# Decay products placed behind the factors' bank, and masks and high parts reordered, in two recurrent layers

## The chip, the cores and the metric

The kernel runs on one core of a Trainium2 chip. The metric is the device time of one execution in microseconds (us), lower is better. Five engines work side by side, each in its own program order, and meet only at semaphores: PE (TensorE, matrix products into eight PSUM banks), ACT (ScalarE), DVE (VectorE), POOL (GpSimd) and SP, which issues the weight transfers.

## The reference

A sequence of 256 tokens of width 1024 goes through four layers (a recurrent mixer, stick-breaking attention, sparse attention, a recurrent mixer again), each with a gated feed-forward block, and then through two hybrid attention layers. All is in float32. The change lies in the recurrent mixer, which runs twice, in layer 0 (n = 0) and layer 3 (n = 1):

```python
def rwkv7_time_mix(h, v_first, mix, w_rkv, ..., v_res):
    shifted = jnp.pad(h, ((0, 0), (1, 0), (0, 0)))[:, :-1]
    xm = h[:, :, None, :] + (shifted - h)[:, :, None, :] * mix
    rkv = jnp.einsum('bsjd,jde->bsje', xm[:, :, :3], w_rkv)
    r, k, v = rkv[:, :, 0], rkv[:, :, 1], rkv[:, :, 2]
    ...
    if v_res is not None:
        v0, v1, v2 = v_res
        v = v + (v_first - v) * jax.nn.sigmoid(v0 + (xv @ v1) @ v2)
    ...
    def step(state, inp):
        r_t, w_t, k_t, v_t, kk_t, a_t = inp
        sa = jnp.einsum('bhvk,bhk->bhv', state, kk_t)
        state = (state * w_t[:, :, None, :]
                 - sa[..., None] * (kk_t * a_t)[:, :, None, :]
                 + v_t[..., None] * k_t[:, :, None, :])
        return state, jnp.einsum('bhvk,bhk->bhv', state, r_t)
```

## The kernel before

The recurrence is computed in four chunks of 64 tokens. For each chunk and head the kernel builds a 64 x 64 lower triangular matrix from products of decayed keys and inverts it by doubling: blocks of 2, 4, 8, 16 and 32 (LEVELS). Around this work stand the three big products with `w_rkv`, in the order keys (m = 1), queries (m = 0), values (m = 2). Every weight block of 256 columns is used as a high and a low part: ACT rounds the high part (`hi`, line 444), DVE subtracts for the low part (`lo`, line 454), PE multiplies with both (lines 384 to 386). The inputs of these products are split the same way. For the values' input DVE mixes tokens into the slots of buffer 12 (`prepare(2, ...)`, line 2355), ACT rounds them (`rounded(2, ...)`, line 1589: the high parts) and DVE subtracts (line 2241).

The order on each engine is written out by hand, and each engine works strictly in it. Around the change it is as follows.

- PE: third queries' block `full(0, 1, 2)`; the gate's and the values' factors "gv" (lines 772 and 773), which ACT reads out with a sigmoid (line 1687) and, in layer 3, a copy (line 1689); the decay products "pb" (line 790, one pair of banks for each j of 0 and 1); the first half of the fourth queries' block; the decay products "bp" (line 790 again, operands exchanged); the second half of that block; then for each level first products "xs" (line 814) and transposes "turn" (line 823), half a block of the values, second products "low" (line 814), the other half. The first products need "bp" as ACT has copied it (line 1701) and the triangle as DVE has masked it (line 2469).
- DVE: the decayed keys (lines 2395 and 2396), which "pb" multiplies; two low parts; the values' mixed input; the four masked copies of "pb" into the triangle (line 2469); low parts.
- ACT: two high parts of weights; the third queries' block out of its bank (line 1597); the sigmoid; the four high parts of the values' input; the four copies of "bp"; high parts; the fourth queries' block; then the copies of "xs" (line 1710) and of "turn" (line 1701), the latter into buffer 12.

PSUM banks go round a ring. `bank(e, key, *free)` takes the next and makes PE wait for what frees its last content. From "pb" to the end of the inversion the ring has banks 1 to 7 (`cur["first"] = 1`), and bank 0 is kept for the blocks of queries and values. `cur["bank"]` is set to the bank after which the ring goes on. Behind the inversion it goes over all eight again, from the bank after the last one used.

The lines that set the place of "pb" and that take a bank:

```python
            i = cur["first"] + cur["bank"] % (8 - cur["first"])
            cur["bank"] += 1
            for ev in bank_free.get(i, ()):
                e.wait_ge(*at(*ev))
...
            cur["first"], cur["bank"] = 1, bank_of["full", n, 0, 2]
            for j in range(2):
                gram("pb", j, Pm, Bt_)
```

Of the kernel before, what the change touches and what calls it, by code (L numbers as in the profile page):

```python
# [88 lines left out]
class Book:  # L89
# [8 lines left out]
    def up(self, name, *keys):  # L98
        self.n[name] += 1
        for k in keys:  # L100
            self.value[name, k] = self.n[name]
        return self.sems[name], 1
# [7 lines left out]
    def at(self, name, key):  # L110
        return self.sems[name], 1 if self.rehearsal else self.value[name, key]
# [9 lines left out]
def build(nc, A, out_ap, OFF, NCONST):  # L121
    ctx = ExitStack()
    with ctx:
# [13 lines left out]
        BUF = {}  # L137
# [3 lines left out]
        HH, HL, XH, XL, XHe, XLe = (t[:, i, :] for t in (H_, X_, E_) for i in range(2))  # L141
# [16 lines left out]
        up, at, mark = book.up, book.at, book.mark  # L158
# [6 lines left out]
        def C(name, a=0, b=None):  # L165
            o, n = OFF[name]
            return CT[:, o + a:o + (n if b is None else b)]
# [4 lines left out]
        def FM(i):  # L172
            return BUF[i][:, :].rearrange("p (k t) -> p k t", k=KD)

        def TM(i):
            return BUF[i][:, :].rearrange("p (j c) -> p j c", j=2)
# [4 lines left out]
        def low8(m):  # L181
            return C(f"low{m}").bitcast(I32).unsqueeze(1).to_broadcast([P, 8, HD])

        def q8(ap):
            return ap.rearrange("p (q t) -> p q t", q=8)
# [18 lines left out]
        def pair(t, g):  # L204
            return FR(t)[:, 2 * g:2 * g + 2, :]
# [102 lines left out]
        cur, bank_of, bank_free = {}, {}, {}  # L308

        def PS(*key):  # L310
            return PSB[bank_of[key]]
# [126 lines left out]
        def hi(e, count=2):  # L438
            for u in range(cur["hi"], min(cur["hi"] + count, len(units))):
                j, k0, kn = units[u]  # L440
                e.wait_ge(s_raw[j % RAW], landed[j])
                if u >= UNITS:
                    e.wait_ge(book.sems["unit"], u - UNITS + 1)
                e.activation(wh[:, u % UNITS, 0:kn * 256], raw[:, j % RAW, k0 * 256:(k0 + kn) * 256], ACT.Copy).then_inc(*up("hi"))  # L444
                cur["hi"] = u + 1

        def lo(e, count=2):
            for u in range(cur["lo"], min(cur["lo"] + count, len(units))):
                j, k0, kn = units[u]
                e.wait_ge(book.sems["hi"], u + 1)  # L450
                e.wait_ge(s_raw[j % RAW], landed[j])
                if u >= UNITS:
                    e.wait_ge(book.sems["unit"], u - UNITS + 1)
                e.tensor_tensor(wl[:, u % UNITS, 0:kn * 256], raw[:, j % RAW, k0 * 256:(k0 + kn) * 256],  # L454
                                wh[:, u % UNITS, 0:kn * 256].bitcast(F32), ALU.subtract).then_inc(*up("lo"))
                cur["lo"] = u + 1
# [33 lines left out]
        def col(name, k, a=0):  # L490
            c = COL[name] + a * KD + k
            return cols[:, c:c + 1]
# [57 lines left out]
        def mix_slot(g):  # L550
            return FM(12)[:, 2 * (g % 2):2 * (g % 2) + 2, :]
# [165 lines left out]
        def pe_rwkv(e, layer, n):  # L717
# [9 lines left out]
            def block_halves(m, p, g):  # L727
                key, free = ("full", n, m, g), ("dve", ("vmix", n, g)) if n and m == 2 else ("act", ("full", n, m, g))
                ready = [[("dve", ("xml", n, m, k // 2))] for k in range(KD)] if g == 0 else None
                o = kept_bank(e, 0, key, free)  # L730
                for k0, kn, u in next_units(KD):
                    fm_unit(e, key, o, KD, k0, kn, u, parts_of(*((HH, HL), (XH, XL))[p]), ready)
                    yield
# [72 lines left out]
            groups = [(j, par) for j in range(2) for par in range(2)]  # L806
# [46 lines left out]
                    i.then_inc(*up("mm", ("v2", n, g)))  # L853

            last_read = block_halves(0, 1, 3)
            cur["first"], cur["bank"] = 1, bank_of["full", n, 0, 2]
            for j in range(2):
                gram("pb", j, Pm, Bt_)
            next(last_read)
# [719 lines left out]
        def act_rwkv(e, layer, n):  # L1579
# [5 lines left out]
            def rounded(m, hi_, g, *free):  # L1585
                for ev in free:
                    e.wait_ge(*at(*ev))
                e.wait_ge(*at("dve", ("xm", n, m, g)))
                e.activation(pair(hi_, g), mix_slot(g), ACT.Copy).then_inc(*up("act", ("xmh", n, m, g)))
# [97 lines left out]
            e.activation(sg[0:32, 1, :], PS("gv", n)[0:32, 0:S], ACT.Sigmoid).then_inc(*up("act", ("gv", n)))  # L1687
            if n:
                e.activation(lor[32:64, :], PS("gv", n)[32:64, 0:S], ACT.Copy).then_inc(*up("act", ("gv", n)))
            for g in range(4):  # L1690
                rounded(2, HH, g, ("unit", ("full", n, 1, 3)))
            term, V = FM(4), TM(2)
            Y, pTM, bTM, kTM = FM(6), TM(3), TM(1), TM(8)
            Lk, Un, Tt, At = (BUF[b][:, :].rearrange("p (j r x) -> p j r x", j=2, r=2) for b in (14, 0, 12, 1))
# [2 lines left out]
            groups = [(j, par) for j in range(2) for par in range(2)]  # L1697

            def copy_out(key, dst, scale=1.0):
                e.wait_ge(*at("mm", key))  # L1700
                e.activation(dst, PS(*key)[:, :], ACT.Copy, scale=scale).then_inc(*up("act", key))
# [5 lines left out]
            def quarters_out(key, m, j, dst, scale=1.0):  # L1707
                for a in range(2):
                    e.wait_ge(*at("mm", (key, n, m, j, 1)))
                    e.activation(dst[:, j, :, a, :], q8(PS(key, n, m, j, a)[:, :]), ACT.Copy, scale=scale).then_inc(*up("act", (key, n, m, j, a)))  # L1710

            def turned(m):
                for j in range(2):
                    for r in range(2):
                        copy_out(("turn", n, m, j, r), Tt[:, j, r, :])

            for j, par in groups:
                copy_out(("bp", n, j, par), At[:, j, par, :])
            hi(e, 1)
            for g in range(4):  # L1720
                hi(e, 1)
                if g == 0:
                    evac(0, 3, R_)
                elif n == 0:
                    evac(2, g - 1, v_)
                for j in range(2):
                    quarters_out("xs", LEVELS[g], j, X1)
                turned(LEVELS[g] // 2)
                if g == 2:
                    e.wait_ge(*at("mm", ("gv", n)))  # L1730
                    e.wait_ge(*at("dve", ("PB", n, 1)))
                    e.activation(BUF[0][:, :].rearrange("p (q t) -> p q t", t=HD), C("eye").unsqueeze(1).to_broadcast([P, 32, HD]),
                                 ACT.Copy).then_inc(*up("act", ("eye", n)))
                hi(e, 1)
                if n and g == 0:
                    for q in range(4):
                        sigmoids("v2", q, "rw_v0", vmix, 0)
# [585 lines left out]
        def dve_rwkv(e, layer, n):  # L2323
# [17 lines left out]
            def prepare(m, hl, *free):  # L2341

                def rest(g):
                    dve_lo_part(e, mix_slot(g), (pair(hl[0], g), pair(hl[1], g)), ("act", ("xmh", n, m, g)), ("xml", n, m, g))

                for ev in free:
                    e.wait_ge(*at(*ev))
                for g in range(4):
                    e.wait_ge(*at("dve", ("step", n, g)))
                    e.wait_ge(*at("act", ("d0", n, g)))  # L2350
                    if g >= 2:
                        e.wait_ge(*at("dve", ("xml", n, m, g - 2)))
                    for u in range(2):
                        k = 2 * g + u
                        i = e.scalar_tensor_tensor(out=mix_slot(g)[:, u, :], in0=d[:, k, :], scalar=col("rw_mix", k, n * 6 + m), in1=h[:, k, :],
                                                   op0=ALU.mult, op1=ALU.add)
                    i.then_inc(*up("dve", ("xm", n, m, g)))
                    if g:
                        rest(g - 1)
                rest(3)  # L2360
# [92 lines left out]
            erase_and_write(0)  # L2453
            erase_and_write(1)
            lo(e)
            prepare(2, (HH, HL), ("unit", ("full", n, 1, 3)), ("dve", ("k2", n, 3)))
            BR, KR, Lk, Un = (BUF[b][:, :].rearrange("p (j r x) -> p j r x", j=2, r=2) for b in (9, 11, 14, 0))
            T, Xw = GQ(6), GQ(0)
# [2 lines left out]
            def masked(kind, j, par, dst, name):  # L2461
                e.wait_ge(*at("mm", (kind, n, j, par)))
                e.tensor_tensor(q8(dst[:, j, par, :]), q8(PS(kind, n, j, par)[:, :]), bc8(name), ALU.mult).then_inc(*up("dve", (kind, n, j, par)))

            groups = [(j, par) for j in range(2) for par in range(2)]
            for j, par in groups:
                e.wait_ge(*at("act", ("minus eye", n, j)))
                e.wait_ge(*at("mm", ("pb", n, j, par)))
                e.copy_predicated(q8(BUF[6][:, (2 * j + par) * 512:(2 * j + par) * 512 + 512]), low8(1),
                                  q8(PS("pb", n, j, par)[:, :])).then_inc(*up("dve", ("pb", n, j, par), ("low", n, 1, j, par)))  # L2470

            def level(key, m, dst):
                for j in range(2):
# [698 lines left out]
```

## Time and profile before

| | |
|---|---|
| median of 3 runs | 1830.6 us (1829.88 to 1832.39) |
| the profiled execution | 1837.71 us |
| its span, first to last instruction | 1835.9 us |
| mean granted PE clock | 0.984 |
| busy: PE, DVE, ACT, POOL | 1762.6, 1288.7, 1034.0, 69.2 us |

The span is 1.8 us short of that execution's own time, and the execution is 0.4% above the median of the runs. A timeline lists instructions in order of time, equal ones merged into one row with a count: start, length from the first's start to the last's end, engine, line, operation, output and inputs, and in brackets the idle time of the engine before it with what ended it. The ends of PE's instructions are modelled, and successive ones overlap.

### The profile page before, as it was taken

To read this page: it belongs to the slowest core of one execution; us is meant where nothing else is said; L and a number is where in the kernel's file an instruction comes from. 1 tells how busy PE (TensorE), PEld (TensorE's weight loads), DVE (VectorE), ACT (ScalarE), POOL (GpSimd) and SP (SyncE) were. 2 spreads that over 40 slices of the span, in tenths; PEclk is the share of its full clock that TensorE was granted. 3 is DMA by queue.
4 is the path that set the end of the run, shared out by engine and by line. 5 is a ranking of instruction groups with operands and counts; after the bars stand their busy time and mean duration, and the time that the engine had idled before them with its cause. 6 is when DMAs were issued, how large, how long until landed. Compare 5 with 4: busy or idle time off the path is not lost.

```text
span 1835.9 us, 40364 instructions
## 1 busy us (share of the span) xinstructions
PE 1762.6 (96%) x17129; PEld 1594.8 (87%) x17129; DVE 1288.7 (70%) x1897; ACT 1034.0 (56%) x1608; POOL 69.2 (4%) x54
## 2 busy tenths in 40 slices
PE   7899899999999999999999999899999999998997
PEld 6798798889989888987888889798798888997997
DVE  7853468965457995598788757663579956875874
ACT  6856365554556555456655548754555544564564
POOL 0001000000000000214000000001000000000000
PEclk9999999999999999999999999999999999998998
DMA  7320157755436875542495653210368655453541
GB/s 222 119 86 4 52 183 253 251 190 181 138 115 229 275 234 179 161 141 79 143 267 188 200 173 115 85 49 4 103 226 278 225 182 167 138 161 103 159 144 64
DMA packets 276298, 287.60 MB, mean 157 GB/s; under 512 B 15304, under 2 KB 261944, under 8 KB 276120
## 3 DMA queue, kind: packets, MB, share of 16 engines
q1 hardware_dynamic: 272824, 283.92, 47.8%
q8 instruction: 136, 2.23, 0.5%
q10 hardware_dynamic: 3296, 1.11, 0.3%
q14 instruction: 42, 0.34, 0.1%
HBM read 283.96 MB, written 1.05 MB: 155 GB/s over the span
## 4 chain that ended last, share of the span: by engine, by line
PE 89%; DVE 5%; ACT 3%; issue 2%; DMA 0%; SPq 0%; DVEq 0%; ACTq 0%
PE ps L407 24%; PE ps L408 13%; PE ps L384 10%; PE ps L385 9%; PE ps L386 9%; PE ps L814 2%; PE ps L422 2%; PE ps L423 2%; PE ps L424 2%; PE ps L790 1%; PE ps L799 1%; DVE wl L454 1%; PE ps L983 1%; PE ps L714 1%; PE ps L634 1%
## 5 line engine op out<-in xcount | busy, mean ns | idle before, releaser
L454 DVE TENSOR_TENSOR wl<-raw,wh 128x1024 fp32r<-128x1024 f32 x484 | 582.3, 1227 | 243.7 <-ACT wh L444 240.9
L444 ACT ACTIVATE wh<-raw 128x1024 fp32r<-128x1024 f32 x484 | 497.4, 1041 | 376.6 <-PE ps L408 189.8
L407 PE MATMUL ps<-HH,wh 128*128 128x512 f32 x1408 | 490.8, 391 | 0.8 <-DVE HH L2870 0.8
L408 PE MATMUL ps<-HH,wl 128*128 128x256 f32 x1408 | 397.0, 282 | 0.0
L407 PEld LDWEIGHTS ps<-HH,wh 128*128 128x128 f32 x1408 | 264.3, 188 | 56.4 <-DVE HH L2870 1.1
L384 PE MATMUL ps<-HH,wh 128*128 128x256 f32 x928 | 269.3, 290 | 6.9 <-DVE HH L2672 6.4
L408 PEld LDWEIGHTS ps<-HH,wl 128*128 128x128 f32 x1408 | 266.1, 189 | 0.1
L386 PE MATMUL ps<-HH,wl 128*128 128x256 f32 x928 | 261.4, 282 | 0.8 <-issue 0.8
L385 PE MATMUL ps<-HH,wh 128*128 128x256 f32 x928 | 261.6, 282 | 0.0
L384 PEld LDWEIGHTS ps<-HH,wh 128*128 128x128 f32 x928 | 177.0, 191 | 15.8 <-DVE HH L2672 4.9
L385 PEld LDWEIGHTS ps<-HH,wh 128*128 128x128 f32 x928 | 177.1, 191 | 1.3 <-issue 1.2
L386 PEld LDWEIGHTS ps<-HH,wl 128*128 128x128 f32 x928 | 177.0, 191 | 1.0 <-issue 1.0
L384 PE MATMUL ps<-XH,wh 128*128 128x256 f32 x512 | 146.9, 287 | 10.5 <-DVE XH L2241 6.9
L385 PE MATMUL ps<-XH,wh 128*128 128x256 f32 x512 | 144.6, 282 | 0.0
L386 PE MATMUL ps<-XH,wl 128*128 128x256 f32 x512 | 144.3, 282 | 0.0
L407 PE MATMUL ps<-XE,wh 128*128 128x512 f32 x336 | 117.0, 390 | 0.0
L384 PEld LDWEIGHTS ps<-XH,wh 128*128 128x128 f32 x512 | 97.8, 191 | 14.1 <-DVE XH L2241 6.5
L385 PEld LDWEIGHTS ps<-XH,wh 128*128 128x128 f32 x512 | 97.9, 191 | 0.0
L386 PEld LDWEIGHTS ps<-XH,wl 128*128 128x128 f32 x512 | 97.9, 191 | 0.0
L408 PE MATMUL ps<-XE,wl 128*128 128x256 f32 x336 | 94.8, 282 | 0.0
L422 PE MATMUL ps<-wh,HH 128*128 128x256 f32 x256 | 74.9, 293 | 0.0
L3052 POOL TENSOR_TENSOR B<-B 128x512 f32<-128x512 f32 x20 | 26.0, 1301 | 1294.4 <-ACT B L1499 1294.3
(337 smaller groups left out, 3090.4 us busy)
## 6 DMA issues: line engine op xcount, KB each, us to landing
raw<-in_ffn_w_gu_dram SPq DMA_DIRECT2D x88, 1024.0 KB, 5.3
raw<-in_ffn_w_down_dram SPq DMA_DIRECT2D x32, 1024.0 KB, 5.2
raw<-in_w_in_dram SPq DMA_DIRECT2D x32, 1024.0 KB, 5.5
raw<-in_rw_w_rkv_dram SPq DMA_DIRECT2D x24, 1024.0 KB, 5.2
B<-in_w_ada_dram SPq DMA_DIRECT2D x24, 1024.0 KB, 7.5
raw<-in_ds_w_in_dram SPq DMA_DIRECT2D x14, 1024.0 KB, 5.2
raw<-in_ffn_w_down_dram SPq DMA_DIRECT2D x16, 768.0 KB, 4.4
raw<-in_sb_w_qkv_dram SPq DMA_DIRECT2D x12, 1024.0 KB, 5.2
```

The costliest lines, as they stand in the source:

```text
L384: e.matmul(om, h_[:, k, c], xh_, start=m == 0 and k0 + k == 0, stop=False, skip_group_check=True)
L385: e.matmul(om, h_[:, k, c], xl_, start=False, stop=False, skip_group_check=True)
L386: i = e.matmul(om, l_[:, k, c], xh_, start=False, stop=k0 + k == kt - 1, skip_group_check=True)
L407: e.matmul(o[:, m, :], h_[:, k, c], x_, start=k0 + k == 0, stop=False, skip_group_check=True)
L408: i = e.matmul(o[:, m, 0:S], l_[:, k, c], x_[:, 0, :], start=False, stop=k0 + k == kt - 1, skip_group_check=True)
L422: e.matmul(oj, xh_[:, c], h_[:, k, :], start=j == 0 and k0 + k == 0, stop=False, skip_group_check=True)
L423: e.matmul(oj, xl_[:, c], h_[:, k, :], start=False, stop=False, skip_group_check=True)
L424: i = e.matmul(oj, xh_[:, c], l_[:, k, :], start=False, stop=k0 + k == KD - 1, skip_group_check=True)
L444: e.activation(wh[:, u % UNITS, 0:kn * 256], raw[:, j % RAW, k0 * 256:(k0 + kn) * 256], ACT.Copy).then_inc(*up("hi"))
L454: e.tensor_tensor(wl[:, u % UNITS, 0:kn * 256], raw[:, j % RAW, k0 * 256:(k0 + kn) * 256], wh[:, u % UNITS, 0:kn * 256].bitcast(F32), ALU. ...
L814: i = e.matmul(os[a][half(b), q * HD:q * HD + HD], L[half(a), j, q, b, :], Rr[half(a), j, q, b, :], start=True, stop=True, skip_group_chec ...
L3052: e.tensor_tensor(SQ[:, 0:2, :], SQ[:, 0:2, :], SQ[:, 2 * g:2 * g + 2, :], ALU.add).then_inc(*up("pool", ("sq", tag, g)))
```

## The change

Four edits, all for both recurrent layers. On PE the ring of banks goes on behind the bank of "gv" and no longer behind that of the third queries' block. On DVE the four masked copies of "pb" stand ahead of the values' mixed input and no longer behind it. On ACT the third and the fourth high part of that input stand between the copies of "bp" and no longer ahead of them. And ACT waits for the last low part of that input before its first copies into buffer 12, whose slots the mixed input uses.

```diff
@@ PE, pe_rwkv
             last_read = block_halves(0, 1, 3)
-            cur["first"], cur["bank"] = 1, bank_of["full", n, 0, 2]
+            cur["first"], cur["bank"] = 1, bank_of["gv", n]
             for j in range(2):
                 gram("pb", j, Pm, Bt_)
             next(last_read)
@@ ACT, act_rwkv
                 e.activation(lor[32:64, :], PS("gv", n)[32:64, 0:S], ACT.Copy).then_inc(*up("act", ("gv", n)))
-            for g in range(4):
-                rounded(2, HH, g, ("unit", ("full", n, 1, 3)))
+            rounded(2, HH, 0, ("unit", ("full", n, 1, 3)))
+            rounded(2, HH, 1, ("unit", ("full", n, 1, 3)))
...
             for j, par in groups:
+                if j:
+                    rounded(2, HH, 2 + par, ("unit", ("full", n, 1, 3)))
                 copy_out(("bp", n, j, par), At[:, j, par, :])
             hi(e, 1)
             for g in range(4):
...
                 for j in range(2):
                     quarters_out("xs", LEVELS[g], j, X1)
+                if g == 0:
+                    e.wait_ge(*at("dve", ("xml", n, 2, 3)))
                 turned(LEVELS[g] // 2)
@@ DVE, dve_rwkv
             erase_and_write(0)
             erase_and_write(1)
             lo(e)
+            groups = [(j, par) for j in range(2) for par in range(2)]
+            for j, par in groups:
+                e.wait_ge(*at("act", ("minus eye", n, j)))
+                e.wait_ge(*at("mm", ("pb", n, j, par)))
+                e.copy_predicated(q8(BUF[6][:, (2 * j + par) * 512:(2 * j + par) * 512 + 512]), low8(1),
+                                  q8(PS("pb", n, j, par)[:, :])).then_inc(*up("dve", ("pb", n, j, par), ("low", n, 1, j, par)))
             prepare(2, (HH, HL), ("unit", ("full", n, 1, 3)), ("dve", ("k2", n, 3)))
...
-            groups = [(j, par) for j in range(2) for par in range(2)]
-            for j, par in groups:
-                e.wait_ge(*at("act", ("minus eye", n, j)))
-                e.wait_ge(*at("mm", ("pb", n, j, par)))
-                e.copy_predicated(q8(BUF[6][:, (2 * j + par) * 512:(2 * j + par) * 512 + 512]), low8(1),
-                                  q8(PS("pb", n, j, par)[:, :])).then_inc(*up("dve", ("pb", n, j, par), ("low", n, 1, j, par)))
```

## Rows read from the trace of the kernel before

**Rows 1.** The page, chain that ended last, share of the span by engine.

```profile
PE 89%; DVE 5%; ACT 3%; issue 2%; DMA 0%; SPq 0%; DVEq 0%; ACTq 0%
```

**Rows 2.** PE's waits: line <- engine and line waited for: us in total, times, longest.

```profile
PE ps L790 <- ACT lor L1689: 5.5, 1, 5.5
PE ps L790 <- ACT sg L1687: 4.8, 1, 4.8
```

**Rows 3.** Timeline of PE in layer 0, from "gv" to the values' first half.

```profile
81.17 0.59 PE L773 MATMUL ps<-lor,CT 64*32 64x255 f32 x2
86.57 3.69 PE L790 MATMUL ps<-B 64*64 64x64 f32 x128 [4.81 <-ACT sg L1687]
...
94.05 2.10 PE L790 MATMUL ps<-B 64*64 64x64 f32 x128
96.08 0.39 PE L384 MATMUL ps<-XH,wh 128*128 128x256 f32 x1
...
99.08 2.22 PE L814 MATMUL ps<-B 64*64 64x64 f32 x128
101.23 1.97 PE L823 MATMUL ps<-CT,B 128*128 128x128 f32 x16
102.95 0.37 PE L384 MATMUL ps<-HH,wh 128*128 128x256 f32 x1
```

**Rows 4.** Timeline of PE in layer 3, "gv", "pb" and "bp".

```profile
1162.34 0.59 PE L773 MATMUL ps<-lor,CT 128*64 128x255 f32 x2
1168.44 3.69 PE L790 MATMUL ps<-B 64*64 64x64 f32 x128 [5.51 <-ACT lor L1689]
...
1175.98 2.09 PE L790 MATMUL ps<-B 64*64 64x64 f32 x128
```

**Rows 5.** Windows: length, each engine's busy us (instructions), granted clock, DMA share, GB/s.

```profile
81.76:86.57 4.81, 0.00 (x1) 0.00 (x0) 3.46 (x6) 4.78 (x7) 0.00 (x0) 0.87 0.33 115
86.57:90.19 3.62, 3.62 (x128) 3.50 (x128) 2.85 (x6) 1.62 (x3) 0.00 (x0) 0.50 0.41 142
90.19:92.20 2.01, 2.01 (x13) 2.01 (x10) 1.86 (x4) 0.63 (x1) 0.00 (x0) 0.52 0.00 0
94.05:99.08 5.03, 5.03 (x153) 4.83 (x152) 3.30 (x4) 3.01 (x5) 0.00 (x0) 1.00 0.26 74
...
1195.42:1200.84 5.42, 5.42 (x25) 5.20 (x24) 1.01 (x1) 0.84 (x2) 0.00 (x0) 0.50 0.00 0
```

**Rows 6.** Timeline of ACT in layer 0.

```profile
79.81 0.58 ACT L1597 ACTIVATE B<-ps 128x512 f32<-128x512 f32 x1
...
82.37 1.99 ACT L444 ACTIVATE wh<-raw 128x1024 fp32r<-128x1024 f32 x2
84.26 0.58 ACT L1597 ACTIVATE B<-ps 128x512 f32<-128x512 f32 x1
84.85 1.28 ACT L1687 ACT_TABLE_LOAD   x1
86.15 0.37 ACT L1687 ACTIVATE sg<-ps 32x256 f32<-32x256 f32 x1
...
95.27 2.06 ACT L1701 ACTIVATE B<-ps 128x512 f32<-128x512 f32 x4 [4.15 <-PE ps L790]
```

**Rows 7.** Timeline of DVE in layer 0.

```profile
80.15 1.22 DVE L2396 TENSOR_TENSOR B<-B 128x1024 f32<-128x1024 f32 x1
...
83.56 1.66 DVE L2355 SCALAR_TENSOR_TENSOR B<-B,cols 128x256 f32<-128x256 f32 x4
87.07 0.69 DVE L2241 TENSOR_TENSOR HH<-B,HH 128x512 fp32r<-128x512 f32 x1 [1.85 <-ACT HH L1589]
...
91.76 2.58 DVE L2469 COPY_PREDICATED B<-CT,ps 128x512 f32<-128x512 int32 x4
```

**Rows 8.** Timelines of DVE and of ACT in layer 3, one row of each.

```profile
1161.62 1.21 DVE L2396 TENSOR_TENSOR B<-B 128x1024 f32<-128x1024 f32 x1
...
1168.02 0.38 ACT L1689 ACTIVATE lor<-ps 32x256 f32<-32x256 f32 x1
```

## The prediction

> **What bounds the kernel now.** I read the page first, then PE's own list of waits, then the timelines of PE, ACT and DVE around the one place that the diff touches, and last the clock of that place. PE carries 89% of the chain that ended last [rows 1]: only time that PE stands idle, or runs at its lower clock, can be won by moving work on the other engines. The list of PE's waits has the place of the diff twice, once in each recurrent layer: the decay products of line 790 wait 4.8 us in layer 0 (n = 0) and 5.5 us in layer 3 (n = 1), for ACT [rows 2]. In PE's timeline of layer 0 the product ahead of it (line 773) ends at 81.76, and "pb" starts at 86.57 [rows 3]. Its 128 instructions then take 3.69, where the same form ("bp", same line) takes 2.10 at 94.05. The granted clock explains that: 0.87 over the idle stretch, 0.50 (the 1.2 GHz level) over "pb", 0.52 over the first 2 us of the half block behind it [rows 5]. So the stall costs its own length and slow products after it.
>
> What PE waits for is a PSUM bank, not data. Both inputs of "pb" are ready when DVE ends line 2396 at 81.37 [rows 7], 0.39 before PE is free. Its first bank was that of "gv" (bank 6, counting the program's allocations; 6 again in layer 3). That is freed by ACT's sigmoid of line 1687, which starts at 86.15 because it stands in order behind two weight copies, the copy of a block at 84.26 and a table load [rows 6]. In layer 3 a further copy (line 1689, 1168.02 and 0.38 long) ends the wait [rows 8].
>
> **The change, step by step (layer 0).** No instruction is added or taken away on any engine, and no DMA; one wait is added on ACT. All terms are moves.
>
> *The bank.* The ring now starts behind "gv": "pb" takes 7, 1, 2, 3, "bp" takes 4, 5, 6, 7. Bank 7's last reader is ACT's copy of the second block, 79.81 plus 0.58 [rows 6]; banks 1 to 3 were read by the key norms before that. So "pb" starts where "gv" ends. I take 81.7, as products in a run start a little before the modelled end of the one ahead. From [rows 3], start to start: "pb" 2.03 (94.05 to 96.08), a half block 3.00 (96.08 to 99.08). "bp" then starts at 81.7 + 2.03 + 3.00 = 86.73 instead of 94.05: **7.32 us** earlier. Of this 4.81 is the stall and the rest the clock, which has no reason to fall when PE doesn't stop. "bp" needs bank 5, free at 84.84, and for its second pair bank 6 at 87.75, free when the sigmoid ends at 86.52 [rows 6]. So the wait on "gv" is there still, 1.2 us clear.
>
> *The masks ahead of the mixed input.* DVE's four masked copies (2.58 together) moved from 91.76 to where the mixed input started, 83.56 [rows 7]. The first pair of "pb" is done at 82.8 and the second at 83.8, so DVE doesn't stand: it masks from 83.6 to 86.0. Behind them are queued the mixed input, two low parts of weights and everything later on DVE. The mixed input moves back by less than 2.5: before, DVE stood 1.85 waiting for ACT's first high part [rows 7], which waited for the sigmoid; now the first pair is mixed at 86.9, when ACT is just free, and the high part waits for DVE instead. From the first low part on everything is some 0.6 later than before, and the mixed input ends at 92.4. PE wants it for the values' first half block, at 86.73 + 2.03 + 3.00 + 3.87 = 95.6 (3.87 is 99.08 to 102.95 [rows 3]), with the weights' low parts, done at 93.5 and 94.7. About 1 us clear.
>
> *ACT's order.* High parts 0 and 1 run at 87.0 and 87.7, "bp" copies 0 and 1 (0.5 each, four in 2.06 [rows 6]) at 88.3, high part 2 when DVE has mixed it (89.5), copy 2 at 90.1, high part 3 at 91.1, copy 3 to 92.2. PE's first products start at 91.76 with the first two copies and need the last two at 92.8: clear by 0.6. Then ACT has two weight copies (1.99 a pair), one block and four copies of first products [rows 6]: the first of those ends near 95.2. PE turns four groups from 93.91, 0.43 apart (1.72 for 16 [rows 3]); the fourth takes that copy's bank at 95.2. This is the next late thing: I take 0.2 us of new stall (0 to 0.6). Before, ACT stood waiting for PE there and had over 1 us to spare. The turned copies end at 97.6 and 98.5; PE wants the pairs at 98.6 and 99.7.
>
> *The new wait.* ACT's wait for the mixed input (over at 92.4) stands ahead of the turned copies, reached at 96.6: nothing. Behind it queue those copies and the next weights' high parts. With the cover gone each microsecond that the mixed input comes after 96.6 delays PE's second products by about as much.
>
> *Layer 3.* The same sum: "gv" ends at 1162.93 and "pb" may start near 1162.9 (DVE's products end at 1162.83 [rows 8]); "bp" starts at 1162.9 + 5.03 = 1167.9 instead of 1175.98 [rows 4]: **8.1 us**. ACT is later by the extra copy, so the fourth turned group may wait 0.3 (0 to 0.8).
>
> *The banks afterwards.* Every later bank in a layer is one further on. Owners and order stay the same, except that bank 0 (the values' last block) falls to another of the next transposes, which wait for that block anyway. In layer 0 the feed-forward blocks begin at an even bank, 4 in both cases; in layer 3 they begin two banks later, on banks long read. I cost it at nothing (0 to 0.5).
>
> **Sum.** 7.3 - 0.2 + 8.1 - 0.3 = 14.9, rounded to 15 us, of the profiled execution of 1837.7 (span 1835.9). Behind these places PE is fed by engines that mostly wait for PE, so the gain should go through to the end. The runs' median is 1830.6, 0.4% below; that is 0.06 us on 15. Forecast **1830.6 - 15.1 = 1815.5**.
>
> **Rivals.** (a) *The clock falls anyway*, for as long as it did before: "gv" and "pb" now stand together, 3 us of narrow products. Against it: "bp", half block, first products and turned ones ran at 1.00 throughout. For it: in layer 3 the half block behind the values' rates (line 852) ran at 0.50 [rows 5], though PE's list shows no wait ahead of the rates. Then only the stalls go, 4.8 + 5.5 = 10.3: **1820.3**. The Trainium skill has such a case: "TensorE: Matmul & The Clock Gate", section "A second HAM failure mode: psum-queue depth-cycling", tells of a kernel whose short stops between groups of products, as it went round the banks, made the clock swing between its levels. By that rule the time would be this rival's; the clock of 1.00 over the groups from 94.05 to 99.08 speaks against it.
>
> (b) *ACT becomes the next wait*: its copies come 2 to 4 us per layer late at the turned groups. The order above leaves hardly any slack there. The gain falls to 7 to 11: **1821.6**.
>
> (c) *The change doesn't do what it says*: "pb" goes on waiting for ACT, if my count of banks is wrong. The pairs of "pb" then come at 88.4 and 90.2 (86.57 and 3.69 in two halves), DVE's masks end near 91.5 and hold the mixed input up to 97.9 (6.4 as above), the weights' low parts to 100.3; PE wants them at 102.95: still hidden. **1830.6**.
>
> (d) *Slower*: the clock falls at "pb" and stays at 1.2 GHz through "pb", half, "bp", half, first products and turned groups, 13.9 us at full clock. "pb" shows the price of half clock, 1.6 for 2.1; on the whole stretch 13.9 x 1.6 / 2.1 = 10.6 a layer against 7.3 and 8.1 won: **1836.4**. It decides when more than some 10 us of this stretch run slow. Against it: no row shows the low level for so long.
>
> **How the numbers follow.** Forecast 0.77, (a) 0.09, (b) 0.07, (c) 0.04, (d) 0.03. The forecast's own band is 1812.7 to 1818: no new stall, less the 2.5 between the runs shown, up to the three new stalls at their upper bounds (0.6, 0.8, 0.5: 1817.1) and 1 us for the stops that the chain calls issue [rows 1]. The range reaches on to (a) and the middle of (b), which leaves out some 0.15: **1812.7 to 1822.0**. What a measurement of this kernel can tell from no change is about 0.2%, 3.7 us. Faster by more: 0.93; within: 0.04, from (c); slower: 0.03, from (d).
>
> **What the profile will show.** Right: PE's list has no wait of line 790 for ACT above 0.5, "pb" takes near 2.1 and the clock is 1.00 over it; "bp" starts 7.3 and 8.1 earlier, counted from the end of "gv"; DVE masks ahead of the mix with no idle above 0.5. The thin spots would show as PE waiting at the turned groups (line 823) for ACT, or at the values' first half block for DVE. The clock at 0.50 after "gv" with no stop would prove (a); a wait of line 790 that is left, (c).

## The result, and the profile after

The changed kernel takes 1821.66 us (median, 1820.53 to 1824.41) beside 1831.44 us for the kernel before: ratio 0.9949, 95% interval 0.9933 to 0.9965, a gain of 6.4 to 12.3 us. Two further comparisons below gave 0.9940 (0.9925 to 0.9955) and 0.9928 (0.9908 to 0.9949). Over all executions of the comparisons the mean is 1833.5 us before (68 executions, standard error 0.3) and 1821.2 us after (14, 0.8): 12.4 us. One further execution of the changed kernel took 3483.94 us, at a granted clock of 1.00; it counts as slow and is in no mean, median or ratio here, and what held it up is not known. The profiled execution of after took 1820.53 us, its span is 1818.7 us. The forecast was a gain of 15.1 us, to 1815.5.

PE in layer 0 first, from "gv" to the values' first half block (the lines that answer to [rows 3]; start, length, engine, line, operation, output and inputs, count, idle before it):

```profile
80.60 0.59 PE L773 MATMUL ps<-lor,CT 64*32 64x255 f32 x2
81.12 2.10 PE L790 MATMUL ps<-B 64*64 64x64 f32 x128
83.15 0.39 PE L384 MATMUL ps<-XH,wh 128*128 128x256 f32 x1
...
86.15 2.10 PE L790 MATMUL ps<-B 64*64 64x64 f32 x128
...
91.18 2.22 PE L814 MATMUL ps<-B 64*64 64x64 f32 x128
93.33 1.97 PE L823 MATMUL ps<-CT,B 128*128 128x128 f32 x16
95.05 0.37 PE L384 MATMUL ps<-HH,wh 128*128 128x256 f32 x1
```

The idle bracket at "pb" is gone, and it takes 2.10 instead of 3.69. From "gv" to "bp" it is 86.15 - 80.60 = 5.55 us; before it was 94.05 - 81.17 = 12.88. Layer 3, beside [rows 4], has 1162.65 - 1157.07 = 5.58 instead of 13.64:

```profile
1157.07 0.59 PE L773 MATMUL ps<-lor,CT 128*64 128x255 f32 x2
1157.60 2.10 PE L790 MATMUL ps<-B 64*64 64x64 f32 x128
...
1162.65 2.10 PE L790 MATMUL ps<-B 64*64 64x64 f32 x128
```

The windows of after over "pb", the half block and "bp" (columns as in [rows 5]) show the clock at its upper level; before, it was 0.87 over the idle stretch, 0.50 over "pb" and 0.52 over the start of the half block:

```profile
80.60:83.15 2.55, 2.55 (x132) 2.07 (x130) 2.55 (x4) 2.49 (x4) 0.00 (x0) 1.00 0.00 0
83.15:86.15 3.00, 3.00 (x31) 2.87 (x25) 3.00 (x6) 2.83 (x4) 0.00 (x0) 1.00 0.61 189
86.15:91.18 5.03, 5.03 (x154) 4.83 (x153) 4.65 (x10) 3.98 (x8) 0.00 (x0) 1.00 0.29 102
```

DVE, then ACT, in layer 0 after ([rows 6 and 7] before):

```profile
83.04 2.58 DVE L2464 COPY_PREDICATED B<-CT,ps 128x512 f32<-128x512 int32 x4
85.52 1.66 DVE L2359 SCALAR_TENSOR_TENSOR B<-B,cols 128x256 f32<-128x256 f32 x4
...
91.23 0.69 DVE L2245 TENSOR_TENSOR HH<-B,HH 128x512 fp32r<-128x512 f32 x1 [0.16 <-ACT HH L1589]
```

```profile
86.47 0.63 ACT L1589 ACTIVATE HH<-B 128x512 fp32r<-128x512 f32 x1 [0.47 <-DVE B L2359]
...
91.10 0.58 ACT L1701 ACTIVATE B<-ps 128x512 f32<-128x512 f32 x1
91.58 2.00 ACT L444 ACTIVATE wh<-raw 128x1024 fp32r<-128x1024 f32 x2
93.47 0.59 ACT L1597 ACTIVATE B<-ps 128x512 f32<-128x512 f32 x1
93.95 2.06 ACT L1710 ACTIVATE B<-ps 128x512 f32<-128x512 f32 x4
95.86 2.10 ACT L1701 ACTIVATE B<-ps 128x512 f32<-128x512 f32 x4
```

This trace reaches "gv" 0.57 us earlier than that of before (80.60 instead of 81.17), so 0.57 is added to its times when they are held against the working. The masks start with no idle time. The mixed input ends at 91.92, which makes 92.5 where 92.4 was worked out; ACT's last copy of "bp" ends at 91.68 (92.25 for 92.2), and the turned copies start at 95.86 (96.4 for 96.6). So the place itself came out as worked out, step by step. What was not worked out stands 17 and 21 us behind the start of "bp" in PE's timeline, in two stops that the profile calls issue (it finds no releaser):

```profile
102.97 0.39 PE L384 MATMUL ps<-HH,wh 128*128 128x256 f32 x1 [0.78 <-issue]
104.23 2.09 PE L814 MATMUL ps<-B 64*64 64x64 f32 x116
107.08 0.45 PE L814 MATMUL ps<-B 64*64 64x64 f32 x12 [0.76 <-issue]
```

In PE's list of waits the kernel before has one such stop between 70 and 160 us, which the changed kernel has as well (us, times, longest):

```profile
PE ps L386 <- issue: 0.8, 1, 0.8
```

To see which stretches differ at all, the starts of the same PE instructions were subtracted in the timelines of several executions. In us, start to start:

| stretch of PE's work | before, 3 executions | after, 4 executions | difference of the means |
|---|---|---|---|
| layer 0, "gv" to "bp" | 12.88, 12.38, 13.10 | 5.55, 5.54, 5.55, 5.54 | -7.2 |
| layer 0, "bp" to line 714 | 60.81, 60.88, 60.83 | 63.02, 62.40, 62.77, 62.63 | +1.9 |
| layer 0, line 714 to the first feed-forward block | 93.93, 92.58, 93.88 | 92.37, 92.34, 90.02, 93.13 | -1.5 |
| layer 3, "gv" to "bp" | 13.64, 12.42, 12.98 | 5.57, 5.57, 5.55, 5.55 | -7.5 |
| layer 3, "bp" to line 714 | 70.39, 70.26, 69.18 | 70.29, 70.67, 70.41, 70.41 | +0.5 |
| layer 3, line 714 to the fourth feed-forward block | 90.56, 90.27, 88.73 | 87.33, 87.82, 88.77, 89.77 | -1.4 |
| first feed-forward block to the first product of line 1160 | 512.59 in all three | 512.58 to 512.60 | 0.0 |
| line 1160 to the third feed-forward block | 145.00, 146.86, 146.84 | 146.98, 144.99, 144.98, 145.09 | -0.7 |

The four rows of the stretches that the change touches, "gv" to "bp" and "bp" to line 714, add up to -12.3 us, beside 12.4 between the means of all executions. That the two agree is in part chance: the whole spans of these same traces differ by 16.7 us (1835.4 and 1818.7 on average), since the profiled executions of before (1837.71, 1839.69 and 1834.15 us) lie above the mean of that kernel. The other 4.4 lie in stretches that differ by 1 to 4 us from execution to execution within either kernel. They go with the clock: its lower level covers 59.7, 59.7 and 59.8 us of the traces of before and 42.5, 39.1, 42.6 and 49.5 of those of after, in many places of the program.

### The profile page after: what moved, and what is told of

Read it like the earlier page. It is cut to its first block, busy times and chain, and to the rows that moved or that the text cites. A ratio compares the mean times of both kernels' runs of the same rounds, so it can differ in the third digit from the quotient of the medians.

```text
span 1818.7 us, 40366 instructions
## 1 busy us (share of the span) xinstructions
PE 1757.0 (97%) x17129; PEld 1588.2 (87%) x17129; DVE 1288.5 (71%) x1897; ACT 1034.0 (57%) x1608; POOL 69.1 (4%) x54
## 4 chain that ended last, share of the span: by engine, by line
PE 91%; DVE 5%; ACT 2%; issue 2%; DMA 0%; SPq 0%; DVEq 0%; ACTq 0%
PE ps L407 24%; PE ps L408 13%; PE ps L384 10%; PE ps L386 9%; PE ps L385 9%; PE ps L814 2%; PE ps L422 2%; PE ps L424 2%; PE ps L423 2%; PE ps L790 1%; PE ps L799 1%; PE ps L823 1%; PE ps L714 1%; DVE wl L454 1%; PE ps L634 1%
## 5 line engine op out<-in xcount | busy, mean ns | idle before, releaser
L384 PEld LDWEIGHTS ps<-HH,wh 128*128 128x128 f32 x928 | 177.5, 191 | 16.7 <-issue 6.4
```

The lines of the kernel that those rows point to most:

```text
L384: e.matmul(om, h_[:, k, c], xh_, start=m == 0 and k0 + k == 0, stop=False, skip_group_check=True)
```

## The experiments

**Theories.** A: the gain is the two stops plus the low clock behind them, 15 us, and something new takes a part of it back. B: only the stops are worth time (10.3 us), since half-clock stretches removed here come back elsewhere.

**The same kernels again.** No edit, for further traces and for the clock of each execution.

> The kernel before, unchanged, for a second trace and for the granted clock of several executions. If the half clock at the stall is a steady cost, every execution has a mean clock near 0.984 and the time stays 10 us above that of the changed kernel with the same clock. If half-clock stretches come and go elsewhere in the program, the mean clock varies from run to run by 0.001 to 0.003 and the span with it, by some 2 to 5 us, and the first profile (span 1835.9, six us over the median) was one with many of them. The stalls of 4.8 and 5.5 us at line 790 are there in either case.

Measured: ratio 0.9997 (0.9985 to 1.0008). The mean granted clock went from 0.982 to 0.987 over 64 executions of the kernel before, and the span with it. In layer 3 of this trace the low stretch covered only a part of "pb" (timeline of PE, then the window of the stretch, columns as in [rows 5]):

```profile
1167.13 0.59 PE L773 MATMUL ps<-lor,CT 128*64 128x255 f32 x2
1173.24 3.35 PE L790 MATMUL ps<-B 64*64 64x64 f32 x128 [5.51 <-ACT lor L1689]
1179.55 2.09 PE L790 MATMUL ps<-B 64*64 64x64 f32 x128
```

```profile
1172.70:1176.10 3.40, 2.86 (x108) 2.86 (x112) 2.09 (x4) 2.04 (x5) 0.00 (x0) 0.51 0.54 186
```

The stop is 5.51 again, but "gv" to "bp" takes 12.42 and not 13.64. The stop is a fixed cost, the clock behind it is not.

> The kernel before, once more, for a third trace. The stop at line 790 of 4.8 and 5.5 us is the same in every execution. The half-clock stretch that begins at it is 3.4 or 6.8 us long, so that the time from the factors to the exchanged products is 12.4 to 12.9 us in layer 0 and 12.4 to 13.6 in layer 3. If instead the clock falls fully each time, it is 12.9 and 13.6 in this trace too.

Measured: 1834.15 us, 13.10 us in layer 0 (0.2 above the range expected) and 12.98 in layer 3. With 5.55 for the products and 4.8 to 5.6 for the stop, the clock cost 2.5, 2.0 and 2.7 us in layer 0 of the three executions and 2.6, 1.3 and 1.8 in layer 3: on average 4.3 for both layers, where one execution had shown 5.1.

> The changed kernel, unchanged, for a second trace. Both theories expect no wait of line 790 for ACT and 2.1 us for its products at full clock in both layers. If only the stalls are worth time, the ratio is 0.9944 (10.3 us of 1831); if the clock's part of 2.5 us a layer is won too, 0.9917 (15.3 us).

Measured: ratio 0.9940 (0.9925 to 0.9955). The value for the stalls alone lies in this interval, that with the whole part of the clock does not. No wait of line 790 for ACT; the two issue stops are there with 0.39 and 0.50.

> The changed kernel, once more, for a third trace. From the factors to the exchanged products 5.55 and 5.57 us as in the first two. If the two stops called issue behind it in layer 0 belong to the changed kernel, they are there again, 1 to 1.6 us together; if they were chance, they are not.

Measured: 1817.95 us and, in PE's timeline, the same two stops a third time:

```profile
103.35 0.38 PE L384 MATMUL ps<-HH,wh 128*128 128x256 f32 x1 [0.50 <-issue]
107.46 0.45 PE L814 MATMUL ps<-B 64*64 64x64 f32 x12 [0.77 <-issue]
```

**The clock alone.** The stall is filled with products that nobody reads (into bank 0), so the wait stays and the clock should not fall:

```diff
             last_read = block_halves(0, 1, 3)
+            for _ in range(5 + n):
+                e.matmul(PSB[0][:, :], C("bones"), h[:, 0:2, :], start=True, stop=True, skip_group_check=True)
             cur["first"], cur["bank"] = 1, bank_of["full", n, 0, 2]
```

> The kernel before, with 5 (layer 0) and 6 (layer 3) products of 128x128 by 512 columns put between the factors and the decay products, into bank 0, which nobody reads then: 0.9 us each, they fill the stall and keep PE busy, while the wait for ACT's sigmoid stays. If half clock behind the stall costs 2.5 us a layer for good, this kernel is 5 us faster than the kernel before (ratio 0.9973). If the half-clock stretches only move to other places of the program, it is within 1 us of the kernel before (ratio 0.9995 to 1.0005). In its trace the decay products take 2.1 us instead of 3.7 in both cases.

Measured: 1829.85 us, ratio 0.9982 (0.9970 to 0.9993), 1.3 to 5.5 us faster than before, for a kernel that does more. PE's timeline in layer 0 and the window from "pb" on:

```profile
80.82 4.56 PE L857 MATMUL ps<-B,CT 128*128 128x512 f32 x10
85.70 2.09 PE L790 MATMUL ps<-B 64*64 64x64 f32 x128 [0.32 <-ACT sg L1689]
90.72 2.16 PE L790 MATMUL ps<-B 64*64 64x64 f32 x128
```

(Line 857 is the filling; the trace has two records for each of its products.)

```profile
85.70:92.00 6.30, 6.30 (x233) 6.10 (x237) 5.38 (x10) 2.32 (x5) 0.00 (x0) 1.00 0.25 86
```

Counted from "gv", "pb" starts when it started before (5.4 us behind it), and it takes 2.09; the mean clock of 12 executions is 0.988, as after the change, against 0.985. So B falls: the clock behind the stop is worth 1.3 to 5.5 us, and about as much in the traces (4.3).

**The bank alone.** Only the line of the bank is changed:

```diff
-            cur["first"], cur["bank"] = 1, bank_of["full", n, 0, 2]
+            cur["first"], cur["bank"] = 1, bank_of["gv", n]
```

> The bank alone: the decay products go behind the factors' bank, DVE's masks and ACT's high parts stay where they were. The products start at 81.7 in layer 0. The second pair of the exchanged products needs the bank that DVE's first mask frees, and that mask stands behind the mixed input until about 92.5: PE stops there for about 4.6 us. Expected by the order worked out from rows: 2 to 3 us a layer won, ratio 0.997 to 0.998, less whatever the clock does at the new stop. If instead the bank was all that held PE, the ratio is that of the whole change, 0.994 to 0.995.

Measured: ratio 0.9992 (0.9984 to 1.0001). PE's timeline, then DVE's:

```profile
80.99 2.09 PE L790 MATMUL ps<-B 64*64 64x64 f32 x128
86.02 1.16 PE L790 MATMUL ps<-B 64*64 64x64 f32 x64
91.94 1.99 PE L790 MATMUL ps<-B 64*64 64x64 f32 x64 [4.76 <-ACT B L1701]
```

```profile
91.12 2.54 DVE L2469 COPY_PREDICATED B<-CT,ps 128x512 f32<-128x512 int32 x4
```

That is less than the 2 to 3 us a layer that were expected: at most 2.9 us for both layers together. The stop only moved from "pb" to the second pair of "bp", with the same length. The profile names ACT, but the program makes that pair wait for bank 7, which held the first pair of "pb" and which the first mask frees, and that mask (91.12 and about 0.7) ends just ahead of 91.94. ACT's two copies before that (line 1701) end at 91.0 and 91.4. The masks' new place is a condition of the gain and no gain by itself.

**The order alone.** The changed kernel with the line of the bank as it was:

```diff
-            cur["first"], cur["bank"] = 1, bank_of["gv", n]
+            cur["first"], cur["bank"] = 1, bank_of["full", n, 0, 2]
```

> The changed kernel with the old bank for the decay products: PE waits for ACT's sigmoid again, while the masks stand ahead of the mixed input and ACT's last two high parts between its copies. The working from rows says that the later mixed input is still hidden: within 1 us of the kernel before (ratio 0.9995 to 1.0005). If the masks in front of the mixed input hold up the values' product, it is 2 us or more slower. PE's stream of instructions is that of the changed kernel with the 4.8 us stop put back. If the two stops called issue that the changed kernel has 20 to 25 us behind the decay products (0.4 to 0.8 us each, in layer 0) come from PE no longer standing still there, they are gone in this trace and the stretch from the exchanged products to the transposes of line 714 takes 60.9 us as before; if they come from the new order on ACT and DVE they stay, and it takes 62.4 to 63.

Measured: ratio 1.0009 (0.9997 to 1.0022). "pb" waits for the sigmoid again, and the new order behind it costs nothing that could be measured. PE's whole list of waits from 70 to 160 us (us, times, longest):

```profile
PE ps L790 <- ACT sg L1687: 4.8, 1, 4.8
PE ps L386 <- issue: 0.6, 1, 0.6
PE ps L790 <- DVE B L2479: 0.3, 1, 0.3
```

The stops at lines 384 and 814 are gone, and "bp" to line 714 takes 61.02. PE's instructions are those of the changed kernel but for the numbers of banks. So these stops come with PE no longer standing still at "pb", not with the new order on DVE and ACT. That PE is kept busy is not enough for them: in the kernel with the filled stall, where it is, they are missing too, and the first stop, of 1.45 us, comes 40 us behind "bp", where the other kernels have theirs of line 386.

**ACT's order.** The changed kernel with the four high parts together:

```diff
-            rounded(2, HH, 0, ("unit", ("full", n, 1, 3)))
-            rounded(2, HH, 1, ("unit", ("full", n, 1, 3)))
+            for g in range(4):
+                rounded(2, HH, g, ("unit", ("full", n, 1, 3)))
...
             for j, par in groups:
-                if j:
-                    rounded(2, HH, 2 + par, ("unit", ("full", n, 1, 3)))
                 copy_out(("bp", n, j, par), At[:, j, par, :])
```

> The changed kernel with ACT's four high parts of the values' input together again, ahead of the copies of the exchanged products. ACT then reaches those copies only when the fourth high part is done, near 91.7 in layer 0, and the last copy ends near 93.8, while PE could start the first products at 91.8 and needs the last pair of copies at 92.8. Expected: a wait of the first products (line 814) for ACT of about 1 us in each layer, and the turned copies later by 1.6, so 2 to 4 us slower than the changed kernel. If ACT's place between the copies is hidden anyway, no such wait and the same time as the changed kernel (ratio 0.994).

Measured: ratio 0.9948 (0.9933 to 0.9963), beside 0.9940 and 0.9949 for the changed kernel in the two comparisons so far (which was not timed beside it here); intervals of this width neither show nor exclude the 2 to 4 us more that were expected. The first products do wait for ACT's copies, in layer 0 and layer 3:

```profile
93.00 2.21 PE L814 MATMUL ps<-B 64*64 64x64 f32 x128 [1.12 <-ACT B L1701]
...
1171.84 2.37 PE L814 MATMUL ps<-B 64*64 64x64 f32 x128 [1.53 <-ACT B L1701]
```

But in layer 0 the stop of 1.12 takes the place of the two issue stops: neither is left, and "bp" to line 714 takes 62.41, no more than in the changed kernel.

> The changed kernel with ACT's four high parts together, in more rounds. Its waits for ACT (1.1 and 1.5 us) are in the trace, but the issue stops of the changed kernel are not. From the traces: layer 0 takes the same 62.4 us from the exchanged products on, layer 3 takes 1.3 more. Expected: 1 to 1.5 us slower than the changed kernel, ratio 0.0005 to 0.0008 above its. If the waits for ACT cost their full length, 2.6 us, 0.0014 above.

Measured: ratio 0.9940 (0.9925 to 0.9955) beside 0.9928 (0.9908 to 0.9949) for the changed kernel timed together with it. The means of all executions are 1822.5 (10) and 1821.2 (14). The part that ACT's interleaving has in the gain is 1 us or so, and not told from nothing by these runs.

> The changed kernel, timed in more rounds, since the intervals so far reach from 0.9925 to 0.9965. The stretches that the change touches are 12.3 us shorter in three traces against three; if that is the whole effect, the ratio is 0.9933. If the gain of the first sum held (15 us), it is 0.9918; if only the stops are worth time and the new stops called issue take 2 of it, 0.9955.

Measured: ratio 0.9928 (0.9908 to 0.9949), median 1819.68 of five executions. The middle one of the expected values, 0.9933, lies in this interval and at the edge or inside of the other two.

## Why the prediction was right and wrong

Right: what bound the place (PE, by a bank that ACT freed late, not by data), the sign, and nearly every step at the place. "pb" starts 0.52 us behind the start of line 773, the second half of "gv". "bp" comes 7.3 and 8.1 us earlier against the profile that the sum was made on, as worked out to 0.1. DVE doesn't stand ahead of the masks. Bank 6 is free when "bp" needs it. The new wait on ACT costs nothing: the mixed input is done at 91.92 and the turned copies start at 95.86. The later banks show no cost: the 513 us from the first feed-forward block to line 1160 take the same time to 0.02, and no stretch behind line 714 is longer by more than 0.1 on average. One bank is missing from the working: the second pair of "bp" needs bank 7 besides bank 6, and the first mask frees it. The mask's new place does that in time; in the kernel with the bank alone it does not, and PE stops for 4.76 us.

Rival (a) gave 1820.3, near the measured median, yet its mechanism did not happen: the clock over "pb" is 1.00 in every trace of after, and filling the stall alone won time. The rule that the prediction cited beside it, from the Trainium skill, "TensorE: Matmul & The Clock Gate", section "A second HAM failure mode: psum-queue depth-cycling", that short stops between groups of products make the clock swing, shows no effect at this place: over the two new stops of 0.78 and 0.76 us the granted clock stays at 1.00 (102.20 to 109.20 in the trace of after). Rival (b) gave 1821.6, the measured median almost to the digit, and that is luck: its mechanism, copies of ACT that come 2 to 4 us late in each layer at the turned groups, did not happen; they cost nothing in layer 0 and 0.2 us in layer 3. Rival (c) was tried by itself in the kernel with the order alone and came out as priced. For (d) there is no sign in any trace.

Wrong was the size: 15.1 us forecast, 9.8 in the first comparison, 12.4 over all executions, and with it the time, 1821.7 instead of 1815.5. Of these 6.2 us the starting point makes 2.9, the gain 2.7, and the first comparison's four executions of after, whose median is 0.5 above the mean of fourteen, the rest. Three steps failed.

- "*This is the next late thing: I take 0.2 us of new stall (0 to 0.6)*", and 0.3 in layer 3. ACT's copies at the turned groups did come in time (line 823 shows no wait in layer 0, and its row in layer 3 is 2.17 long instead of 1.97). The new stop is another: the issue stops at lines 384 and 814. They make "bp" to line 714 longer by 1.9 us in layer 0, against 0.2 in the sum. (Start to start each costs some 0.3 more than its bracket, since the overlap with the product ahead is lost as well.) Layer 3 is longer by 0.5 there, against 0.3, but that is a mixture: a new stop of 0.71 to 0.99 at line 814 in all four traces of after, one of 1.21 and 1.57 at line 823 in two of the three of before, 0.2 for ACT, and half-clock stretches in both. The prediction had 2% issue in the chain [rows 1] and gave it one microsecond in a bound, as if it were independent of the change. The kernel with the order alone shows that it is not: with the stop put back at "pb", the two stops of layer 0 are gone.
- The clock's part. One execution showed 5.1 us for both layers, three showed 4.3 on average (3.3 to 5.1 at the ends), and the filled stall won 1.3 to 5.5. The sum took a varying cost from a single execution, 0.8 too much.
- The starting point. "*The runs' median is 1830.6*" rests on three executions; the mean of 68 is 1833.5, and single ones lie between 1828.2 and 1839.7. The band below the forecast allowed 2.5 us for that spread, and above it nothing. The 15.1 taken off does not follow from the sum either, which gives 14.9.

With the measured terms the sum is 7.2 - 1.9 + 7.5 - 0.5 = 12.3, against 12.4 (standard error 0.8) over all executions.

What the issue stops wait for can be read from the kept traces: PE's instructions. The profile's page lists a DMA queue of kind instruction, the same for every kernel here (packets, MB, share):

```profile
q8 instruction: 136, 2.23, 0.5%
```

Its packets are of 16 KB each. All 108 stops that the twelve traces call issue for PE, from 0.16 to 1.79 us long, end 1.2 to 1.6 us behind the end of one of these packets; of PE's other instructions at the same lines only 5 to 6% start at such a distance. In the trace of after the packets end at 101.45 and 105.75, and the two stops at 102.97 and 107.08. Counted from the start of "bp", these two packets end 15.2 to 15.3 and 18.9 to 19.6 us behind it in the four traces of after, and 12.8 to 13.7 and 17.3 to 17.9 in those where the two stops are missing and PE does not stop behind the start of "bp" either (the three of before, the order alone, the filled stall). In the kernel with ACT's old order they are as late as in after, but there PE comes over 1 us later too, and the two stops are missing. So with the stop at "pb" PE's instructions came in time, and without it they came late. The stops are not new to the program, either: over a whole trace they add up to 8.2, 6.9 and 7.0 us before and 7.5, 7.8, 7.0 and 8.3 after, as later places have less of them.

What stays open is why these packets come 2 us later behind "bp" when PE has run through. No run changes the supply itself, and in layer 3 a stop ahead does not remove all of them (0.63 us is left at line 823 with ACT's old order).

## What to carry to other kernels

When a stop of the bounding engine is removed, price what that stop was hiding, also on the engine itself: here 14.7 us of stop and clock went, and 1.9 came back in layer 0 as short stops that name no releaser and end with the arrival of PE's instructions. For such a stop, look at the packets of the instruction queue. A cost that rides on the clock should be taken from several executions and counted at its mean. And a wait for a buffer has a next releaser in the same ring: moved by the bank alone, the stop of 4.8 us came back 6 us later at its full length, so the work that frees the next buffer must be moved with it.

## What the runs showed of the hardware that was not expected

- Filling 4.8 and 5.5 us of waiting with 5 and 6 useless products of 0.9 us made the kernel 0.18% faster (0.07 to 0.30%), since the products behind them ran at the upper level of the clock.
- The same stop leads to low stretches of different cover in different executions of the same program: in layer 3 the products of "pb" took 3.69 us in one and 3.35 in another behind the same stop of 5.51.
- From the first feed-forward block to line 1160 PE's timing repeats from execution to execution and from kernel to kernel to 0.02 us in 513; other stretches do not (90.0 to 93.9 us from line 714 to that block).
- PE's stops without a releaser, 0.16 to 1.79 us long and 5.7 to 8.6 us in a trace, end 1.2 to 1.6 us behind a packet of 16 KB of the instruction queue, 108 of 108.
